# Routed experts: three whole 2 MB matrices per block instead of six half matrices

## The reference

```
def expert_block(args):
    xblk, e = args
    hid = jax.nn.silu(xblk @ w_gate[e]) * (xblk @ w_up[e])
    return hid @ w_down[e]
...
out = jnp.zeros((n_tok, d), jnp.float32).at[buf_tok].add(yb.astype(jnp.float32) * buf_w[:, None])
```

## Time and profile before

| | us |
|---|---|
| median of 3 runs | 2854.72 (2854.51 to 2856.84) |
| the profiled execution's own time | 2857.5 |
| its span, first to last instruction | 2855.7 |
| the experts' loop, first gate product to the end of the last down product | about 2204.6 to 2844.7 |

### The profile page before, as it was taken

How to read it: one execution, slowest core, us unless ns; L and a number is a source line. 1 busy time by engine, 2 the same in 40 slices (tenths; PEclk the granted TensorE clock), 3 DMA queues, 4 the chain that set the end, 5 groups by cost and what they waited for, 6 DMA issues and landing times. The chain is left out here.

```text
span 2855.7 us, 42346 instructions
## 1 busy us (share of the span) xinstructions
PE 2713.9 (95%) x17366; PEld 2187.0 (77%) x17366; DVE 1455.8 (51%) x2804; ACT 575.2 (20%) x1121; POOL 0.2 (0%) x4
## 2 busy tenths in 40 slices
PE   8999899999999999999999999999998888888887
PEld 8998799999988999888988998888895323232322
DVE  7768678687555775544345667466323111111112
ACT  1001410010043101122010022344102222222222
POOL 0000000000000000000000000000000000000000
PEclk9999999999999999999999999999998999999999
DMA  7544145364453543545544354454542999999998
GB/s 234 207 162 149 59 150 175 133 206 160 128 141 126 172 174 117 127 115 148 165 155 153 133 133 120 134 149 132 143 142 97 423 422 422 422 422 422 422 422 332
DMA packets 382201, 588.76 MB, mean 206 GB/s; under 512 B 17088, under 2 KB 328672, under 8 KB 348896
## 3 DMA queue, kind: packets, MB, share of 16 engines
q1 hardware_dynamic: 377248, 581.92, 58.3%
q10 hardware_dynamic: 4800, 4.63, 0.5%
HBM read 585.43 MB, written 1.08 MB: 205 GB/s over the span
## 5 line engine op out<-in xcount | busy, mean ns | idle before, releaser
L3285 PE MATMUL bank<-ring,wk 128*64 128x512 f32 x1376 | 313.4, 597 | 52.3 <-DMA ring<-in_w_expert_up 49.8
L3359 DVE TENSOR_TENSOR wk<-bank,wk 64x256 f32<-64x256 f32 x86 | 52.7, 613 | 513.2 <-ACT wk L3319 511.8
L3285 PEld LDWEIGHTS bank<-ring,wk 128*64 128x64 f32 x1376 | 105.2, 137 | 252.5 <-issue 229.4
L844 PE MATMUL bank<-hR,ring 128*128 128x128 f32 x2112 | 267.7, 277 | 3.9 <-DVE hR L426 3.9
L844 PEld LDWEIGHTS bank<-hR,ring 128*128 128x128 f32 x2112 | 253.0, 194 | 4.9 <-DMA ring<-in_ffn_w_in 2.7
L3305 PE MATMUL bank<-ring,wk 128*64 128x512 f32 x688 | 157.1, 598 | 23.7 <-ACT wk L3322 23.7
L1164 PE MATMUL bank<-big,ring 128*128 128x128 f32 x1320 | 159.6, 275 | 0.0
L1164 PEld LDWEIGHTS bank<-big,ring 128*128 128x128 f32 x1320 | 153.5, 192 | 0.1
L733 PE MATMUL bank<-hR,ring 128*128 128x256 f32 x704 | 152.3, 379 | 0.0
L733 PEld LDWEIGHTS bank<-hR,ring 128*128 128x128 f32 x704 | 133.8, 190 | 18.2
L2269 PE MATMUL bank<-big,ring 128*128 128x256 f32 x640 | 141.0, 379 | 1.5 <-ACT big L2833 1.0
(11 more groups left out here) (464 smaller groups left out, 4390.1 us busy)
## 6 DMA issues: line engine op xcount, KB each, us to landing
ring<-in_ffn_w_in SPq DMA_DIRECT2D x88, 1024.0 KB
ring<-in_w_expert_gate SPq DMA_DIRECT2D x86, 1024.0 KB
ring<-in_w_expert_up SPq DMA_DIRECT2D x86, 1024.0 KB
ring<-in_w_expert_down SPq DMA_DIRECT2D x86, 1024.0 KB, 9.0
ring<-in_w_in SPq DMA_DIRECT2D x96, 512.0 KB
ring<-in_ffn_w_out SPq DMA_DIRECT2D x40, 1024.0 KB
ring<-in_w_up SPq DMA_DIRECT2D x22, 1024.0 KB
ring<-in_w_in SPq DMA_DIRECT2D x16, 1024.0 KB
```

The costliest lines, as they stand in the source:

```text
L844: last = nc.tensor.matmul(k.bank[:, 2 * (n % 4) + p // 4, (p % 4) * P:(p % 4 + 1) * P], a[:, c, m * P:(m + 1) * P], b[:, c, :], start=c == ...
L3285: last = nc.tensor.matmul(k.bank[m * SLOTS:(m + 1) * SLOTS, self.GU, :], xg[:, c * SLOTS:(c + 1) * SLOTS], self.piece(2 * h + m)[:, (c % 4 ...
L3359: last = v.tensor_tensor(by_row, up[:, :, 2 * h:2 * h + 2], gate[:, :, 2 * h:2 * h + 2], ALU.mult)
```

## The change

The six pieces become three: gate, up and down, each one transfer of 2 MB into one ring slot, with 4096 floats (16 KB) in each partition. `freed`, `landing` and the ACT and DVE waits count three pieces per block.

PE now takes gate whole and then up whole, into two banks (7 and 4). The two column groups no longer hold gate and up: both are given to the same matrix, group m taking the hidden columns `4p + 2m` and `4p + 2m + 1`. For that the moving operand is read with a step of four floats, `"k (p a) -> k a p"`, 2 x 128 columns of it at a time. So there are 32 products with 256 moving columns where 16 with 512 stood. The put-back of the block before moves between gate and up. `silu` is one operation of 128 x 256 that starts after gate; the multiplication on DVE is one of 128 x 256 with no rearrangement. The bank of up is also the first bank of the transposes.

```diff
-    PIECES = 6
+    PIECES = 3
...
-    GU, TURN, DOWN = 7, (4, 6), 5
+    GATE, UP, TURN, DOWN = 7, 4, (4, 6), 5
...
-        return self.k.ring[:, n // 2, (n % 2) * 2048:(n % 2 + 1) * 2048]
+        return self.k.ring[:, n, :]
...
-            for n, (w, h) in enumerate(((gate, 0), (up, 0), (gate, 1), (up, 1), (down, 0), (down, 1))):
+            for n, w in enumerate((gate, up, down)):
                 sp.wait_ge(k.w_used, self.freed(i, n + 1 - self.PIECES))
-                sp.dma_start(self.piece(n), w[:, h * 2048:(h + 1) * 2048]).then_inc(self.landing(n)[0], 16)
+                sp.dma_start(self.piece(n), w).then_inc(self.landing(n)[0], 16)
...
-            for h in range(2):
-                for m in range(2):
-                    self.arrived(pe, 2 * h + m, i)
-                for c in range(4 * h, 4 * h + 4):
+            for j, bank in enumerate((self.GATE, self.UP)):
+                self.arrived(pe, j, i)
+                for c in range(KC):
+                    w = self.piece(j)[:, c * 512:(c + 1) * 512].rearrange("k (p a) -> k a p", a=4)
                     for m in range(2):
-                        last = nc.tensor.matmul(k.bank[m * SLOTS:(m + 1) * SLOTS, self.GU, :], xg[:, c * SLOTS:(c + 1) * SLOTS],
-                                                self.piece(2 * h + m)[:, (c % 4) * 512:(c % 4 + 1) * 512],
-                                                start=c == 0, stop=c == KC - 1)
-                last.then_inc(k.w_used, 2)
-            pe.wait_ge(self.y_taken, i + 1)
-            pe.wait_ge(self.gw_ready, i + 1)
-            self.put(pe)
+                        last = nc.tensor.matmul(k.bank[m * SLOTS:(m + 1) * SLOTS, bank, 0:256], xg[:, c * SLOTS:(c + 1) * SLOTS],
+                                                w[:, 2 * m:2 * m + 2, :], start=c == 0, stop=c == KC - 1)
+                last.then_inc(k.w_used, 1)
+                if j == 0:
+                    pe.wait_ge(self.y_taken, i + 1)
+                    pe.wait_ge(self.gw_ready, i + 1)
+                    self.put(pe)
...
-            act.wait_ge(k.w_used, self.freed(i, 4))
-            nc.scalar.activation(self.w(self.SI, 512)[SLOTS:P, :], k.bank[0:SLOTS, self.GU, :], ACT.Silu).then_inc(self.silu_ready, 1)
+            act.wait_ge(k.w_used, self.freed(i, 1))
+            nc.scalar.activation(self.w(self.SI, 256), k.bank[:, self.GATE, 0:256], ACT.Silu).then_inc(self.silu_ready, 1)
+            act.wait_ge(k.w_used, self.freed(i, 2))
...
-            for h in range(2):
-                by_row = self.w(self.HI, 256)[h * SLOTS:(h + 1) * SLOTS, :].rearrange("q (a p) -> q p a", a=2)
-                last = v.tensor_tensor(by_row, up[:, :, 2 * h:2 * h + 2], gate[:, :, 2 * h:2 * h + 2], ALU.mult)
-                chain(last, self.hid_ready if h else None)
+            dve.wait_ge(k.w_used, self.freed(i, 2))
+            chain(v.tensor_tensor(self.w(self.HI, 256), k.bank[:, self.UP, 0:256], self.w(self.SI, 256), ALU.mult), self.hid_ready)
```

More of the change, by code:

```diff
@@ L3185, in __init__ @@
         self.route = route
-        self.down_loaded = [k.sem(f"down_loaded{n}") for n in range(2)]
     def arrived(self, eng, n, i):
@@ L3193, in landing @@
     def landing(self, n):
-        if n < NSLOT:
-            return self.k.w_loaded[n], (self.u0 - n + NSLOT - 1) // NSLOT * UNIT_INC
-        return self.down_loaded[n - NSLOT], 0
+        return self.k.w_loaded[n], (self.u0 - n + NSLOT - 1) // NSLOT * UNIT_INC
     def freed(self, i, n):
@@ L3299, in pe @@
             pe.wait_ge(self.ht_taken, i + 1)
-            for h in range(2):
[L3301 to L3307, removed]
+            self.arrived(pe, 2, i)
+            for c in range(4):
+                for m in range(2):
+                    a = c * DM + m * 512
+                    last = nc.tensor.matmul(k.bank[m * SLOTS:(m + 1) * SLOTS, self.DOWN, :], ht[:, c * SLOTS:(c + 1) * SLOTS],
+                                            self.piece(2)[:, a:a + 512], start=c == 0, stop=c == 3)
+            last.then_inc(k.w_used, 1)
         pe.wait_ge(self.y_taken, n + 1)
@@ L3322, in act @@
             nc.scalar.activation(pair(self.w(self.HT, 256)), k.bank[:, self.TURN[0]:self.TURN[1] + 1:2, 0:P], ACT.Copy).then_inc(self.ht_taken, 1)
-            act.wait_ge(k.w_used, self.freed(i, 6))
+            act.wait_ge(k.w_used, self.freed(i, 3))
             nc.scalar.activation(self.w(self.Y, 512), k.bank[:, self.DOWN, :], ACT.Copy).then_inc(self.y_taken, 1)
@@ L3353, in dve @@
         with dve.Fori(0, n) as i:
-            chain.enter(i, 4, [(self.hid_ready, 1), (self.gw_ready, 1)])
+            chain.enter(i, 3, [(self.hid_ready, 1), (self.gw_ready, 1)])
             dve.wait_ge(self.silu_ready, i + 1)
-            gate, up = (ap.rearrange("q (p a) -> q p a", a=4) for ap in (self.w(self.SI, 512)[SLOTS:P, :], k.bank[SLOTS:P, self.GU, :]))
-            for h in range(2):
-                by_row = self.w(self.HI, 256)[h * SLOTS:(h + 1) * SLOTS, :].rearrange("q (a p) -> q p a", a=2)
-                last = v.tensor_tensor(by_row, up[:, :, 2 * h:2 * h + 2], gate[:, :, 2 * h:2 * h + 2], ALU.mult)
-                chain(last, self.hid_ready if h else None)
+            dve.wait_ge(k.w_used, self.freed(i, 2))
+            chain(v.tensor_tensor(self.w(self.HI, 256), k.bank[:, self.UP, 0:256], self.w(self.SI, 256), ALU.mult), self.hid_ready)
             dve.wait_ge(self.put_done, i + 1)
```

## The result

| | us |
|---|---|
| the change, median of 4 runs | 3147.97 (3145.25 to 3152.5) |
| before, median of 4 runs beside it | 2854.93 |
| ratio, 95% interval | 1.1027 (1.1007 to 1.1046) |
| the change's profiled execution, its span | 3152.5, 3150.7 |

The change is slower by 293 us, 10%. That is the place and the price of rival 1 (3070 to 3160 us), not the forecast of 2845.2.

The account below looks back on a forecast made before the run. Weight transfers were taken as the bound, 14.92 us a block. Terms of -8.4, +0.4 and -1.5 us took the profiled 2857.5 to 2848.0, and 2.8 us over the median made it 2845.2; own range 2836 to 2849, full range 2837 to 3130.

Parts of the forecast that it names:

- rival 1: Gate and up: PE becomes the bound by reading with a 16-byte step, 3070 to 3160 us; chance 0.35.
- PE's path, first point: Gate and up on PE: 32 pairs of 256-column matmuls at 0.216 us, 7.01 us with the second start.
- the two far ends: Bounds on the cost of PE's stepped reading of gate and up: 0 and +305 us; 0 was taken.
- The transfers: Weight DMA in mid-loop: 16 KB packets save 0.2 us a block, -8.4 us over 42 blocks, at about 428 GB/s.
- the small ones: Packets under 512 B in the weight transfers: three fewer per block, at up to 9.2 ns each, 0.03 us.
- PE's path without the step: PE's work per block, stepped reading taken as free: 13.80 us, hidden under 14.7 us of transfers.
- The sum: Whole kernel: -8.4 us mid-loop, +0.4 at the start, -1.5 at the end, together -9.5 us.
- the last block's down: End of the loop: down starts 5.1 us after up landed, where before 6.61 were needed; -1.5 us.
- The start: Second block's weight requests: up and down come late, leaving transfer gaps of 0.3 and 0.1 us, +0.4 us.

Follow-up runs that it names:

- the neighbours with pairs: Changed kernel reading two neighbouring columns in turn, PSUM written with the step: each matrix in one transfer (16 KB packets), 2849.02 us, or in two (8 KB), 2857.49 us.
- the contiguous kernel: Changed kernel with each column group reading 256 neighbouring columns instead of a 16-byte step, rearrangement left out: 2849.61 us, ratio 0.9975 to the kernel before.
- the kernel with pairs: Changed kernel with its two moving-column loops exchanged, so neighbouring columns are read in turn and PSUM takes the step: 2849.02 us, ratio 0.9974 to the kernel before.
- the step of 64 bytes: Changed kernel with gate and up columns read in a step of 64 bytes instead of 16, rearrangement left out: 3122.26 us.
- one stepped stream: Changed kernel with the 16-byte step kept in column group 0 only, group 1 reading 256 neighbouring columns: 3166.96 us.
- steps of 8 and 12 bytes: Two versions of the changed kernel reading gate and up columns in a step of 8 or 12 bytes instead of 16: 2850.25 and 2993.4 us.

## Why the prediction was wrong

**The step that failed** is PE's path, first point: "If reading is not slower, a 256-column matmul takes 152.3 us / 704 = 0.216 us", with "I take 0" for the step's cost. It was 7.32 us for gate where 3.5 were put down. Undoing the step alone gives the time back, and so does the exchange of two indices that leaves the same columns for each group. The choice at the two far ends was argued badly: the prediction took the plain matmul for the nearest row since it is the same engine, though that row has no step, and the stepped rows of ACT and DVE had one. These gave the right price, 0.75 to 1.0 ns a column; measured were 1.79 - 0.88 = 0.91. That the size fits so well may be luck: those rows step in what they write, 512 bytes apart, and no run ties their cost to lines.

**Rival 1** had place, mechanism and size: a path of 19.9 to 22.0 us against 21.57, a time of 3070 to 3160 against 3148, SP's queue waiting for PE, the DMA share below 1. It had a chance of 0.35 against 0.44 of the forecast, and the stated range ended at 3130, inside rival 1's times.

**The transfers** were right, seen where PE lets them be. Packets of 16 KB move at 428 to 429 GB/s (forecast about 428); between the neighbours with pairs 6.29 MB / 422 - 6.29 MB / 429 GB/s are 0.24 us a block, where 0.22 for the packets and 0.03 for the small ones were worked out and 0.2 taken. The Trainium skill (DMA: Bandwidth & Descriptors, "Why small descriptors are slow") has a fixed part of about 3 cycles per packet; the prediction's estimate from it, 3.6 us over the loop, is too small for the 8.5 us measured between them.

**PE's path without the step** was 13.80 us in the sum. In the contiguous kernel's second block, where PE waits for no transfer, it is 3.48 + 3.56 + 1.91 + 4.30 + 0.81 us (down with the loop's turn, gate, put-back, up with the multiplication behind it, transposes): 14.06 us from down at 2215.33 to down at 2229.39. That is 0.26 more, over half of it in the put-back, and still under 14.68, so it cost nothing in mid-loop. PE waits 0.39 us per block for gate, not 0.9.

**The sum** of the forecast, -9.5 us, is thus near for the kernel with pairs (7.8 us under the kernel before beside it) and for contiguous columns (7.0 under), and void for the change: with PE as the bound, faster transfers and a shorter end are worth nothing. Of its terms, the last block's down came 5.11 us behind up with contiguous columns (2826.23 to 2831.34; forecast 5.1, before 6.61). The start was put too low at +0.4 us: there PE's longer path is not hidden, and the first down product already comes 12.32 us behind the first gate product, where it was 11.55 before. One reading was off without consequence: the DMA row stands at 9 in eight of the last nine slices and at 8 in the very last.

**The 293 us**: blocks 21.57 - 14.92 = 6.65 us longer, 43 times, are 286. A small rest is down itself: in 4 of 43 blocks it takes 1.7 us longer, together 7 us (last section).

## What to carry to other kernels

Before a moving operand is rearranged in its access pattern, count how many new 16-byte lines it reads per column: at one line a column a float32 matmul runs at half pace here, at two columns a line it loses 4%. Exchange the loops so that neighbours in memory are read one after the other, and let PSUM take the step. And when two rows speak for opposite ends, do not put the price at nothing on a row that lacks the disputed property: here the rows that had a step, though on other engines, gave the better bound.

## What the runs showed that was not expected

PE's writes to PSUM with a step of 16 bytes (3.60 us for gate, 3.61 without) and of 512 bytes (in the kernel with pairs) cost nothing visible, while ACT and DVE pay for a step in SBUF.

In the changed kernel down started at half clock in 4 of 43 blocks, with the step of 64 bytes in 4, with one stepped stream in 12, and in no block of the kernels with contiguous columns, pairs or steps of 8 and 12 bytes. PE in such a block, and the stretches around it:

```profile
2505.52 5.35 PE L3301 MATMUL bank<-ring,wk 128*64 128x512 f32 x16 [0.47 <-ACT wk L3319]
```

```profile
2499.00:2504.00 5.00, 5.00 (x24) 1.53 (x20) 0.00 (x0) 0.00 (x0) 0.00 (x0) 1.00 0.55 229
2504.00:2505.50 1.50, 0.43 (x6) 0.23 (x4) 1.29 (x3) 1.01 (x2) 0.00 (x0) 1.00 0.72 153
2505.60:2508.80 3.20, 3.20 (x8) 0.92 (x10) 0.58 (x3) 0.00 (x0) 0.00 (x0) 0.50 0.79 323
```

The granted clock is 0.50, the 1.2 GHz level, from 2505.6 to 2508.8. Before it fell PE had run stepped matmuls and then little for 1.5 us. The same pause follows the up products in every block of the other kernels without such a fall. The fall was seen only in the three kernels where a column group reads one new line per column, in one profile of each; why there, and why in some blocks and not in all, is open.
